# The state update of an RWKV scan: the old state accumulated in PSUM by identity products instead of a VectorE addition

## What is computed

```python
def step(S, inp):
    w_t, k_t, v_t, kk_t, kka_t = inp[:5]
    S = (S * w_t[:, :, None, :]
         - jnp.einsum('bhij,bhj->bhi', S, kk_t)[..., None] * kka_t[:, :, None, :]
         + v_t[..., None] * k_t[:, :, None, :])
    y = jnp.einsum('bhij,bhj->bhi', S, inp[5]) if emit else None
    return S, y
```

## Time and profile before

| | |
|---|---|
| median of 3 runs | 5619.66 us (5616.84 to 5620.97) |
| profiled execution | 5618.44 us, its span 5616.6 us |
| TensorE (PE) busy in the span | 5215.7 us, 93% |
| VectorE (DVE) busy | 1713.7 us, 31% |
| ScalarE (ACT) busy | 1021.3 us, 18% |
| the stretch of the scan | 1659 to 2420 us, 761 us |

### The profile page before, as it was taken

One profiled execution on the slowest core, in us unless ns is written; L12 is line 12 of the kernel. 1 busy time (PEld: TensorE's weight loads), 2 busy tenths in 40 slices (PEclk: granted clock), 3 DMA queues, 4 the chain that ended last, 5 costly groups with the idle time before them and its releaser, 6 DMA issues.

```text
span 5616.6 us, 60707 instructions
## 1 busy us (share of the span) xinstructions
PE 5215.7 (93%) x26356; PEld 2739.8 (49%) x26356; DVE 1713.7 (31%) x3352; ACT 1021.3 (18%) x2244; POOL 145.1 (3%) x139
## 2 busy tenths in 40 slices
PE   7988999997989999979999999889998999879998
PEld 4554555553447666734443444444443444443443
DVE  3273111116146666521102102661012011581101
ACT  1042100002035555411001000330001000250000
POOL 0000000000000000000000000220000000040000
PEclk8999999998979998889999999869999999959999
DMA  4300121211100000021221222101212222201210
GB/s 196 142 23 30 70 109 76 105 47 43 41 1 3 3 3 2 3 113 60 75 82 56 78 80 75 60 16 60 75 69 74 75 75 78 80 1 59 76 71 26
DMA packets 26745, 338.48 MB, mean 60 GB/s; under 512 B 2896, under 2 KB 2896, under 8 KB 6640
## 3 DMA queue, kind: packets, MB, share of 16 engines
q1 hardware_dynamic: 23792, 324.51, 15.3%
q0 software_dynamic: 2688, 10.09, 0.5%
HBM read 330.40 MB, written 4.19 MB: 60 GB/s over the span
## 4 chain that ended last, share of the span: by engine, by line
PE 86%; DVE 9%; ACT 3%; issue 2%; DMA 0%; SPq 0%; DVEq 0%; ACTq 0%
PE ps L822 68%; PE ps L849 2%; PE ps L1119 1%; PE ps L1050 1%; PE ps L1091 1%; PE ps L950 1%; DVE rstd L1625 1%; PE ps L928 1%; PE ps L1102 1%; PE ps L1181 1%; PE ps L868 1%; DVE arena L1701 1%; PE ps L1040 1%; DVE stat L1727 1%; PE ps L938 1%
## 5 line engine op out<-in xcount | busy, mean ns | idle before, releaser
L822 PE MATMUL ps<-arena 128*128 128x512 f32 (+3 forms) x9728 | 3831.8, 557 | 107.4 <-DVE arena L1822 30.0
L822 PEld LDWEIGHTS ps<-arena 128*128 128x128 f32 x9728 | 1852.2, 192 | 2080.2 <-issue 1647.2
L1267 ACT ACTIVATE square<-arena 128x512 f32<-128x512 f32 (+2 forms) x166 | 107.3, 651 | 1090.6 <-PE ps L849 530.0
L1783 DVE TENSOR_TENSOR arena<-ps,arena 128x512 f32<-128x512 f32 (+1 forms) x136 | 87.6, 644 | 708.8 <-PE ps L822 708.8
L1416 ACT ACTIVATE square<-ps 128x512 f32<-128x512 f32 x88 | 52.6, 598 | 1317.8 <-PE ps L822 1317.8
L849 PE MATMUL ps<-square,ones 128*128 128x512 f32 (+1 forms) x380 | 178.4, 614 | 76.0 <-ACT square L1267 69.7
L1806 DVE TENSOR_TENSOR arena<-ps,square 128x512 f32<-128x512 f32 x88 | 60.9, 692 | 604.8 <-ACT square L1416 604.8
L1795 DVE TENSOR_TENSOR arena<-arena,ps 128x384 f32<-128x384 f32 (+1 forms) x96 | 57.5, 599 | 498.8 <-ACT arena L1400 498.8
L1810 DVE TENSOR_TENSOR arena<-ps,arena 128x512 f32<-128x512 f32 x88 | 60.9, 692 | 470.2 <-PE ps L822 470.2
L1400 ACT ACTIVATE arena<-ps 128x384 f32<-128x384 f32 (+1 forms) x96 | 50.5, 527 | 797.3 <-PE ps L822 797.3
L751 POOL TENSOR_TENSOR arena<-arena 128x512 f32<-128x512 f32 x120 | 136.0, 1154 | 1881.3 <-ACT arena L1330 1881.3
(11 more groups left out here) (216 smaller groups left out, 3544.3 us busy)
## 6 DMA issues: line engine op xcount, KB each, us to landing
arena<-in_panels SPq DMA_DIRECT2D x145, 2048.0 KB, 7.8
arena<-in_panels SPq DMA_DIRECT2D x9, 1536.0 KB, 6.4
arena<-in_bias POOLq DMA_DIRECT2D x8, 512.0 KB, 3.6
arena<-in_x_in SPq DMA_DIRECT2D x1, 3072.0 KB, 10.9
x_save<-arena POOLq DMA_DIRECT2D x1, 2048.0 KB, 7.9
arena<-x_save POOLq DMA_DIRECT2D x1, 2048.0 KB, 28.4
out_x<-arena SPq DMA_DIRECT2D x1, 2048.0 KB, 7.2
arena<-in_mem_in POOLq DMA_DIRECT2D x1, 1024.0 KB, 30.3
```

The costliest lines, as they stand in the source:

```text
L822: ins = pe.matmul(dest, left(k), right(k), start=(k == 0), stop=(k == nk - 1))
L1267: act.activation(square[:, n["sq"] % 2, 0:hi - lo], src(c), ACT.Square).then_inc(sem("square"), one("square"))
L1783: dve.tensor_tensor(Y[:, c, a:b], bank, Y[:, c, a:b], ALU.add).then_inc(sem("tile_free"), one("tile_free"))
```

## The change

Part 2 of a step puts the old state into bank 6 itself. Per direction, two matmuls of a 64 x 64 identity (a diagonal block of the constant `ident`) with the old state open the accumulation, and the two products of L1158 close it. VectorE's addition, its wait for its own write, and the tile `state_sum` go; the multiplication by the decay reads PSUM directly.

```diff
-        state_sum = sb("state_sum", [P, 2, C])
...
                         for d in range(2):
                             q, e, pos, c = place(d, g, s)
                             for h in range(2):
+                                pe.matmul(ps[half(h), 6, (2 + d) * C:(3 + d) * C], ident[half(h), half(h)], state[half(h), buf, d, :],
+                                          start=True, stop=False)
+                            for h in range(2):
                                 ins = pe.matmul(ps[half(h), 6, (2 + d) * C:(3 + d) * C], bkn[par][d][:, 2 * q + e, half(h)],
-                                                uv[par][d][:, q, e, half(h)], start=True, stop=True)
+                                                uv[par][d][:, q, e, half(h)], start=False, stop=True)
                         ins.then_inc(sem("to_state"), one("to_state"))
...
                         dve.wait_ge(sem("to_state"), more("to_state"))
-                        total = state_sum[:, :, :]
-                        settle(dve.tensor_tensor(total, chunked(ps[:, 6, P:2 * P]), state[:, buf, :, :], ALU.add))
                         decay = chunk_decay[:, p % 2, at, :].unsqueeze(2).broadcast_to([P, 2, C])
-                        dve.tensor_tensor(state[:, 1 - buf, :, :], total, decay, ALU.mult).then_inc(sem("state"), one("state"))
+                        dve.tensor_tensor(state[:, 1 - buf, :, :], chunked(ps[:, 6, P:2 * P]), decay, ALU.mult).then_inc(
+                            sem("state"), one("state"))
```

## The result

The changed kernel took 5657.8 us, the median of four runs (5650.89 to 5663.44), against 5620.09 us before (5616.84 to 5620.97). The ratio is 1.0068, with an interval of 1.005 to 1.0085: 37.7 us slower, where 50 were forecast. Its four runs lie in two pairs, 5651 and 5663, and the granted clock over the whole span goes with them: 0.940 and 0.941 in the pair that is faster, 0.937 in the other; before, it was 0.936 in the profiled execution. That pair of numbers turned out to be half of the story.

A forecast was written before the change was run, and what follows sets the result against it. TensorE's list of instructions was taken to bound the scan. Identity products 60.8, less 4.1 at the entry and 5 and 2 of hidden waits, gave +49.7 us, rounded to 50: 5670 us, range 5646 to 5692.

The forecast's parts named there:

- What bounds the scan: In the scan, TensorE's own list of instructions sets the pace, busy 92% of 761 us; the recurrence is hidden.
- The price of the identity products: In part 2, four alternating groups of 0.26 us replace one of 0.38: 0.67 us more per update, 60.8 us in all.
- The share of updates at the low clock: Among the 88 updates, some 6% run at the low clock, where the products add 1.02 us instead of 0.67.
- The lower bound: For an update's four identity products: 0.23 us among their like, 20 us over 88 updates.
- Rival B: In part 2, alternation costs nothing or state products pack beside their neighbours: +9 to +20 us, 5629 to 5640; chance 0.08.
- The entry: Ahead of part 2 in slots 3 and 11, the change of kind is already counted: 46 x 0.09 = 4.1 us off.
- The hidden waits: On TensorE, waits behind part 2 shrink: 5 us off L1091's wait for L1899, 2 us off L1102's for L1480.
- The clock: For the scan, granted clock kept at 0.90, with 0.03 allowed, 17 us to either side.
- Rival C: Scan's granted clock moves; at 0.86 it adds 23 us, +73 in all, 5693, or the other way; bad case chance 0.07.
- The work taken from VectorE: Each of 88 updates loses 0.32 us on VectorE, 28 us, hidden by TensorE's work except where VectorE is late.
- Rival D: VectorE paces the scan, added products run inside waits: -28 us, 5592; chance 0.03 for faster, 0.03 for no change.

The follow-up runs named there:

- one product: Changed kernel with one identity product of 128 rows x 128 columns in place of the four: 5617.48 us against 5616.15 for the kernel before, ratio 1.0002.
- three groups: Kernel before with output products grouped by kind and their state products moved ahead of the product to the state: 5558.58 us against 5615.5, ratio 0.9896.
- the products alone: Kernel before with the four identity products added, written to columns nobody reads, VectorE's addition kept: 5675.26 us against 5615.39, ratio 1.0107.
- The addition alone: Kernel before without VectorE's addition and without identity products, old state left out of the update: 5588.24 us against 5615.39, ratio 0.9949.
- the second one: Kernel before with VectorE's addition made twice per update: 5629.64 us against 5616.15, ratio 1.0026.
- 44 in the second: Changed kernel once more, unaltered, in a comparison of its own with the kernel before: 5663.56 us against 5619.62, ratio 1.0074.
- adding zeros: Kernel before with VectorE's addition replaced by one same-size instruction adding zero times the old state: 5616.3 us against 5617.21, ratio 1.0001.
- the later starts: Changed kernel with five or ten more clearings of a VectorE tile ahead of the scan: 5654.64 and 5657.45 us against 5615.5 for the kernel before.

## Why the prediction was right, and where it was off

*What bounds the scan.* Right. TensorE's list sets the pace: once the clock is taken equal, eight of the ten kernels stand within 2 us of what was forecast from its groups and waits, and the other two (one product, and three groups) 7 and 8 us off, for the reasons given with them.

*The price of the identity products.* Right, and by the row it was taken from: 1.05 us for four alternating groups, seen in the changed kernel, and 53 us at the clock of before for the products alone. The share of updates at the low clock, 6%, was right too: 5 of 88 before, 4 of 88 in the change. The lower bound, 0.23 us for four of one kind, was not reached in the orders tried: four products ahead of a group of their like took 0.28 us, and 0.38 ahead of the other kind. Rival B falls for the code as it is, because the code alternates. The Trainium skill (TensorEngine Tiling (Array Packing), Key Properties) states that a change of the tiling mode drains TensorE. The traces agree with a price on the change: groups of four take 0.28 us where the next one is of their kind and 0.38 where it is not.

*The entry.* Right in size, but counted at twice as many places as there are: L1119 stands ahead of part 2 in slot 3 alone, and there 0.61 us became 0.51 at 20 places and 0.56 at 3. In slot 11 it is L1102, whose 0.45 us did not change. At the 20 places the first group of identity products is also 0.05 us shorter. All this makes some 3 us instead of 4.1.

*The hidden waits.* 13.2 became 9.2 and 3.5 became 1.8: 5.7 us where 7 were forecast. The addition alone was worth 6 at an equal clock, the second one 9. Over the whole scan TensorE's idle time fell by 5.4 us (61.8 to 56.4). With 3 and 5.4 us for these two terms the sum is 52 us, and the changed kernel shows 50 at the clock of before: that the forecast meets it to the microsecond is partly luck, and the 2 us between are not traced.

*The clock.* The direction and the mechanism were right; this is the term of the sum that was mis-sized. I had taken the granted clock of before for the changed kernel and allowed 17 us to either side, which was enough. It rose from 0.90 to 0.93 in one profile and to 0.91 in the other, worth 12 and 2 us in the scan, and 4 and 0.5 us more came off ahead of the scan (1664.1 to 1660.0 and 1663.6). That is the distance between the 5668 forecast on the terms of the profiled execution and the profiled 5652 and 5665. In the median the change cost 38 us in the first comparison and 44 in the second, against 50. Rival C had the mechanism, with the sign that I thought the less important. Its price, 23 us for 0.04 of clock, came out near the 24 that 0.4 us for each of 61 low microseconds give, but not by its working: it took the records of two stretches for work at two clocks, and another stretch of the kernel before holds more records at 0.90 than the one at 0.97, because other work stands in it:

```profile
2284.00:2383.00 99.00, 95.35 (x1952) 73.53 (x1948) 56.19 (x136) 46.54 (x137) 0.00 (x0) 0.90 0.01 3
```

*The work taken from VectorE.* "The work that hides these 28 us is TensorE's" holds for the waits and not for the clock. By itself, the addition taken away gave 27 us, some 22 of clock and the rest of waits and what is not traced. In the change the products came on top and gave most of it back. Rival D named nearly that number with a mechanism that is not there: in the kernel that reached it TensorE waits no less for the state, since it never did, and hardly less for VectorE.

**What stays open** is why the clock does what it does. It is not the numbers (adding zeros kept 0.90). It rose where the addition went, and where groups of products were merged, from 0.90 to 0.94 and 0.96, and not where an addition or alternating products were added alone. The traces show where: the clock falls 19 times in the scan of the kernel before, 16 and 17 times with zeros or a second addition, and 7 times without the addition. Before, it falls at two or three places of each head pair in the middle, and without the addition only at one, within a microsecond of the long wait of L1123. Here is one of the falls that went, some 53 us into a head pair, the 32 us ahead of it and the 12 us behind. Before:

```profile
2076.00:2108.00 32.00, 30.71 (x718) 23.46 (x711) 25.55 (x61) 16.01 (x49) 0.00 (x0) 1.00 0.01 3
2108.00:2120.00 12.00, 12.00 (x184) 10.00 (x181) 3.57 (x10) 6.03 (x17) 0.00 (x0) 0.57 0.01 3
```

The same place without the addition:

```profile
2066.60:2098.60 32.00, 30.60 (x716) 23.33 (x713) 24.08 (x56) 15.87 (x50) 0.00 (x0) 1.00 0.01 3
2098.60:2110.60 12.00, 11.88 (x236) 9.35 (x231) 6.00 (x16) 7.10 (x20) 0.00 (x0) 1.00 0.01 3
```

TensorE did the same work ahead of both, 30.7 and 30.6 us of 32, and the clock fell in one and not in the other. So the work just ahead does not settle it, and when in time the place comes may matter. No run here was made to take that apart, and the later starts above did not control it.

## What to carry to other kernels

Small matmuls are paid by the group of one shape, not by the piece: before adding or moving them, write down where the number of rows of the array changes from one to the next, and put like beside like, in the existing code first. Price a pattern by a row that shows the same pattern, as the outputs did here for the identity products. And where TensorE's clock is not at 1 throughout, compare kernels with the granted clock of the stretch beside the time, since an edit off TensorE's path can move the clock by more than it moves any wait.

## What the runs showed of the hardware that I had not expected

- An instruction of 0.29 us on VectorE, taken out of each of 88 updates, changed TensorE's granted clock in the scan from 0.90 to 0.94 and by it the time by some 22 us, while TensorE's idle time changed by 2 us and its list not at all.
- One fp32 identity product of 128 rows and 128 moving columns takes 0.42 us up to a group with 64 columns; four of 64 x 64 take 0.38.
- The same program falls into executions of 5651 and 5663 us, with whole clocks of 0.941 and 0.937, in one sitting on one chip.
